# Layer 1's gate rows: bias loaded into the gates' own place, two-part rows with one-pass turns, and the eight blocks placed differently around the pooled sums

## The reference

```
def modulation(cond, w_mod, b_mod):
    m = jax.nn.silu(cond) @ w_mod + b_mod
    return jnp.split(m[..., None, :], N_MOD, axis=-1)
...
ml = modulation(c, p["w_mod"], p["b_mod"])
hl = modulate(xl, ml[0], ml[1])
dl = pool_mixer(hl, p)
xl = layer_norm(ALPHA * xl + ml[2] * dl, p["ln1_g"], p["ln1_b"])
fl = sq_relu_mlp(modulate(xl, ml[3], ml[4]), p["w_up"], p["w_down"])
xl = layer_norm(ALPHA * xl + ml[5] * fl, p["ln2_g"], p["ln2_b"])
...
def pool_mixer(h, p):
    u = h @ p["w_in"]
    pooled = multiscale_pool(u).reshape(nb, L, N_POOL_GROUPS, POOL_GROUP_DIM)
    mixed = jnp.einsum('blgc,gce->blge', pooled, p["pool_w"].astype(jnp.float32))
    mixed = mixed.reshape(nb, L, D_MODEL).astype(h.dtype) * p["pool_scale"]
    return mixed @ p["w_out"]
```

## Time and profile before

| | us |
|---|---|
| median of 3 runs | 1493.04 (1492.63 to 1494.13) |
| the profiled execution | 1491.82 |
| its span | 1489.9 |
| PE busy | 1424.0 (96%) |
| PE weight load busy | 1263.0 (85%) |
| DVE busy | 1049.6 (70%) |
| ACT busy | 550.3 (37%) |
| POOL busy | 82.7 (6%) |

### The profile page before, as it was taken

The page is one execution under the profiler, slowest core; times in us unless marked ns, Lnnn a source line. Parts: engine busy times, 40 slices in busy tenths (PEclk is TensorE's granted clock), DMA queues, the critical chain, the costliest instruction groups (busy, mean ns, idle before and its releaser), DMA issues.

```text
span 1489.9 us, 23009 instructions
## 1 busy us (share of the span) xinstructions
PE 1424.0 (96%) x8916; PEld 1263.0 (85%) x8916; DVE 1049.6 (70%) x1686; ACT 550.3 (37%) x993; POOL 82.7 (6%) x145
## 2 busy tenths in 40 slices
PE   4999999899899999999999989989999999999996
PEld 3899998666688988998999879868899899889985
DVE  3694566677667976776776795756797677677678
ACT  3333352266436422332332244443643233223322
POOL 1300000010101000000000010001100000000001
PEclk8999999999999999999999999999999999999998
DMA  9701233586722412312221522561242232223141
GB/s 314 221 29 58 85 120 122 168 273 205 268 85 68 145 57 85 114 60 83 84 85 57 211 75 67 175 202 57 71 142 59 83 114 69 74 84 94 63 167 71
DMA packets 130940, 173.80 MB, mean 117 GB/s; under 512 B 3666, under 2 KB 103370, under 8 KB 130850
## 3 DMA queue, kind: packets, MB, share of 16 engines
q1 hardware_dynamic: 123106, 146.57, 30.6%
q0 software_dynamic: 6928, 23.34, 4.8%
q10 hardware_dynamic: 816, 2.65, 0.5%
HBM read 163.63 MB, written 8.91 MB: 116 GB/s over the span
## 4 chain that ended last, share of the span: by engine, by line
PE 81%; DVE 10%; ACT 3%; issue 3%; DMA 2%; POOL 0%; SPq 0%; ACTq 0%; DVEq 0%
PE ps L721 37%; PE ps L1224 20%; PE ps L703 7%; PE ps L712 6%; PE ps L756 3%; DVE convT L1883 2%; DVE wlo L1797 2%; PE ps L1065 1%; PE ps L1088 1%; DVE acc L2244 1%; PE ps L1076 1%; DMA vec_rows<-in_b_mod_l 1%; DMA raw<-in_w_mod_l 1%; DVE gated L2255 1%; DMA raw_pool<-in_w_out_l 1%
## 5 line engine op out<-in xcount | busy, mean ns | idle before, releaser
L1336 ACT ACTIVATE whi<-raw 128x512 fp32r<-128x512 f32 (+2 forms) x186 | 175.4, 953 | 369.0 <-PE ps L721 307.0
L721 PE MATMUL ps<-whi,hid_hi 128*128 128x512 f32 x640 | 249.6, 390 | 0.0
L721 PE MATMUL ps<-wlo,hid_hi 128*128 128x512 f32 x640 | 249.2, 389 | 0.0
L721 PE MATMUL ps<-whi,hid_lo 128*128 128x512 f32 x640 | 249.0, 389 | 0.0
L1797 DVE TENSOR_TENSOR wlo<-raw,whi 128x512 fp32r<-128x512 f32 (+2 forms) x186 | 201.8, 1094 | 25.2 <-ACT whi L1336 21.6
L2237 DVE TENSOR_TENSOR acc<-acc,ps 128x512 f32<-128x512 f32 x120 | 80.3, 684 | 121.8 <-PE ps L721 121.8
L721 PE MATMUL ps<-whi,h_hi 128*128 128x256 f32 (+1 forms) x480 | 156.8, 327 | 4.6 <-DVE h_lo L2572 2.6
L721 PE MATMUL ps<-whi,h_lo 128*128 128x256 f32 (+1 forms) x480 | 152.9, 318 | 0.0
L721 PE MATMUL ps<-wlo,h_hi 128*128 128x256 f32 (+1 forms) x480 | 152.8, 318 | 0.0
L721 PEld LDWEIGHTS ps<-whi,hid_hi 128*128 128x128 f32 x640 | 120.1, 188 | 25.2 <-DVE wlo L1797 0.8
L721 PEld LDWEIGHTS ps<-whi,hid_lo 128*128 128x128 f32 x640 | 120.2, 188 | 25.0
(11 more groups left out here) (335 smaller groups left out, 2753.2 us busy)
## 6 DMA issues: line engine op xcount, KB each, us to landing
raw<-in_w_mod_l SPq DMA_DIRECT2D x39, 1024.0 KB, 5.3
raw<-in_w_up_l SPq DMA_DIRECT2D x32, 1024.0 KB, 5.6
raw<-in_w_down_l SPq DMA_DIRECT2D x32, 1024.0 KB, 5.0
raw<-in_w_in_l SPq DMA_DIRECT2D x12, 1024.0 KB, 5.3
raw_att<-in_w_mod_l SPq DMA_DIRECT2D x5, 1024.0 KB, 7.5
raw<-in_w_out_l SPq DMA_DIRECT2D x5, 1024.0 KB, 5.0
x_spill<-x_tok POOLq DMA_DIRECT2D x10, 512.0 KB, 3.0
x_tok<-x_spill POOLq DMA_DIRECT2D x10, 512.0 KB, 6.0
```

The lines of the kernel that those rows point to most:

```text
L721: mm = pe.matmul(out, a_of(still, k), w_of(part, k), start=(first and k == 0 and part == 0 and still == 0), stop=(last and k == nk - 1 and ...
L1336: act.activation(ring_piece(whi, w, g), piece(w, g), ACT.Copy).then_inc(hi_done, 1)
```

## The change

- POOL no longer clears and loads `bmod`. Instead it loads the bias of each half of layer 1's gates, broadcast to all partitions, straight into `gate`: two loads of 512 KB behind the token rows' fetch in layer 0's MLP, two behind the norms ahead of layer 1.
- The bias matmul goes. Rows of layer 1's gates are split in two as layer 0's are, with a low half `rowlo[1]` of their own, and turned by four one-pass matmuls. DVE adds the turned row to the bias in `gate`, in place; ACT's copies go.
- A table sets the places: block 40's product at n = 6, turn 40 and product 41 at n = 7, nothing at n = 8 and 9, then one turn and one product each from n = 10 to 15. Turn 47 follows the first token tile of the output projection, and the third tile waits for it.
- DVE has places too: the row difference of block 40 ahead of the last pooled sum, the addition of 40 and the difference of 41 behind it and behind the low part of the sixth sum, and the others behind each low part of the pooled projection.

```
+        TAIL = {6: (None, 40), 7: (40, 41), 10: (41, 42), 11: (42, 43), 12: (43, 44), 13: (44, 45), 14: (45, 46), 15: (46, 47)}
...
+            def preset_gate(half):
+
+                for c in range(2):
+                    pool.dma_start(gate[:, 1 - half, c, :],
+                                   A["b_mod_l1"][(2 + 3 * half) * D:(3 + 3 * half) * D].partition_broadcast(P)).then_inc(ld_gb, 16)
...
                 fetch_x_again(layer)
+                if layer == 0:
+                    preset_gate(0)
...
             norm_share(1)
+            pool.wait_ge(acc_ok[0], 80)
+            preset_gate(1)
...
-                gates = m in gate_blocks and layer == 1
-                if gates:
-                    pe.matmul(ps[0:32, b * 512:b * 512 + BW],
-                              ident[:, 24 * layer + blk:24 * layer + blk + 1].to_broadcast([P, 32]), bmod[:],
-                              start=True, stop=False)
...
-                if m in first_gates:
-                    pe.wait_ge(row_lo, m - first_gates[0] + 1)
+                if m in gate_blocks:
+                    pe.wait_ge(row_lo, m - G0 + 1)
                     pe.wait_ge(mod_out, m)
                     for c in range(2):
-                        for part, rows in enumerate((modrow_r[:, m % 2, :], rowlo[:])):
+                        for part, rows in enumerate((modrow_r[:, m % 2, :], rowlo[m // M_TAIL][:])):
...
-                if m in gate_blocks:
-                    for c in range(2):
-                        mm = pe.matmul(bank(b, c * BW, (c + 1) * BW), selr[:, c, :].bitcast(F32),
-                                       modrow[:, m % 2, :], start=True, stop=True)
...
-                pe.wait_ge(mod_out, M_TAIL if layer == 0 else 48)
+                pe.wait_ge(mod_out, M_TAIL if layer == 0 else 47)
...
                             pe.wait_ge(px_lo, KT)
+                            if t == 1:
+                                mod_turn(47)
+                            if t == 2:
+                                pe.wait_ge(mod_out, 48)
...
             def tail_mods(n):
-                m = M_TAIL + n - 6
-                if M_TAIL < m <= 48:
-                    mod_turn(m - 1)
-                if M_TAIL <= m <= 47:
+                turned, m = TAIL.get(n, (None, None))
+                if turned is not None:
+                    mod_turn(turned)
+                if m is not None:
                     mod_product(m)
...
+            def tail_rows(n):
+                if n in TAIL:
+                    mod_rows(TAIL[n][1])
...
+                    dst = gate[:, 1 - j // 3, :, q * BW:(q + 1) * BW]
+                    bias = gbias[:, j // 3, q * BW:(q + 1) * BW].unsqueeze(1).to_broadcast([P, 2, BW])
+                    dve.tensor_tensor(dst, bank(bk).rearrange("p (c n) -> p c n", c=2), (bias, dst)[layer], ALU.add) \
                         .then_inc(mod_out, 1)
...
                 split_lo(W_OUT[layer] + 1)
                 if layer == 1:
+                    mod_finish(47)
...
+            def tail_gates(n):
+                turned, m = TAIL.get(n, (None, None))
+                if turned is not None:
+                    mod_finish(turned)
+                if m is not None:
+                    row_low(m)
...
             for f in range(KT):
+                if f == 7:
+                    tail_gates(6)
                 pooled(f)
...
+            tail_gates(7)
             pooled_low(KT - 1)
             for f in range(KT):
...
                     .then_inc(px_lo, 1)
+                tail_gates(KT + f)
```

More of the change, by code:

```diff
@@ L133, in build @@
     gate_blocks = [m for m, k in enumerate(mod_k) if (S[k][2] // 4) % 3 == 2]
-    first_gates = [m for m in gate_blocks if S[mod_k[m]][1] == 0]
+    G0 = gate_blocks[0]
     ctx = ExitStack()
@@ L175, in build @@
         modrow = at("modrow", 203.6875, [P, 2, BW])
-        bmod = at("bmod_rows", 205.6875, [P, BW])
         modrow_r = at("modrow_r", 203.6875, [P, 2, BW], F32R)
-        rowlo = at("mod_row_lo", 147, [P, BW], F32R)
+        rowlo = [at(f"mod_row_lo{n}", kb, [P, BW], F32R) for n, kb in enumerate((147, 194.5))]
         selr = at("sel_r", 200.5, [P, 2, P], F32R)
@@ L551, in _ @@
         def _(pool):
-            pool.memset(bmod[:], 0.0).then_inc(zeros, 1)
             pool.memset(cpad[:], 0.0).then_inc(zeros, 1)
             pool.memset(halfp, -0.5).then_inc(zeros, 1)
-            pool.wait_ge(zeros, 1)
-            for l in range(2):
-                pool.dma_start(bmod[24 * l:24 * l + 24, :], A[f"b_mod_l{l}"].rearrange("(b n) -> b n", n=BW)) \
-                    .then_inc(ld_bm, 16)
             for n, name in enumerate(("lam_q1_l0", "lam_k1_l0", "lam_q2_l0", "lam_k2_l0")):
@@ L561, in _ @@
             steps = [0]
-            pool.wait_ge(zeros, 3)
+            pool.wait_ge(zeros, 2)
             def rsqrt(dst, src, n, scale, done):
@@ L738, in mod_product @@
                 b = 6 if m < M_MIX else 7
-                _, layer, blk = S[mod_k[m]]
                 raw_ready(pe, mod_k[m])
@@ L756, in mod_product @@
                     mm = pe.matmul(ps[32 * g:32 * g + 32, b * 512:b * 512 + BW], cpad[:, k, :],
-                                   raw_block(mod_k[m])[:, k * BW:(k + 1) * BW], start=(k < 4 and (k > 0 or not gates)), stop=(k >= 4))
+                                   raw_block(mod_k[m])[:, k * BW:(k + 1) * BW], start=(k < 4), stop=(k >= 4))
                 mm.then_inc(mod_main, 1)
@@ L773, in mod_turn @@
                     pe.wait_ge(mod_out, m)
-                if m >= M_TAIL:
-                    pe.wait_ge(mod_out, m)
-                if m in gate_blocks:
-                    for c in range(2):
-                        mm = pe.matmul(bank(b, c * BW, (c + 1) * BW), selr[:, c, :].bitcast(F32),
-                                       modrow[:, m % 2, :], start=True, stop=True)
-                else:
-                    for n in range(2):
-                        mm = pe.transpose(bank(b, n * P, (n + 1) * P), modrow[:, m % 2, n * P:(n + 1) * P], ident)
+                for n in range(2):
+                    mm = pe.transpose(bank(b, n * P, (n + 1) * P), modrow[:, m % 2, n * P:(n + 1) * P], ident)
                 mm.then_inc(mod_tr, 1)
@@ L1342, in mod_rows @@
                     act.wait_ge(mod_tr, m - 1)
-                act.activation((modrow_r if m in first_gates else modrow)[:, m % 2, :], bank(b, 0, BW), ACT.Copy) \
+                act.activation((modrow_r if m in gate_blocks else modrow)[:, m % 2, :], bank(b, 0, BW), ACT.Copy) \
                     .then_inc(mod_row, 1)
@@ L1702, in _ @@
             last_norms(1, W_IN1)
-            def gate_rows(m):
-                _, layer, blk = S[mod_k[m]]
-                j, q = blk // 4, blk % 4
-                act.wait_ge(mod_tr, m + 1)
-                act.activation(gate[:, 1 - j // 3, :, q * BW:(q + 1) * BW], bank(6).rearrange("p (c n) -> p c n", c=2),
-                               ACT.Copy).then_inc(mod_out, 1)
-            def tail_gates(n):
-                m = M_TAIL + n - 6
-                if M_TAIL <= m <= 47:
-                    mod_rows(m)
-                if M_TAIL < m <= 48:
-                    gate_rows(m - 1)
+            def tail_rows(n):
+                if n in TAIL:
+                    mod_rows(TAIL[n][1])
             def evac_u(f, hf):
@@ L1745, in _ @@
                     split_hi(W_IN1 + (f + 3) // 2)
-                tail_gates(f)
+                tail_rows(f)
             pool_high(KT - 1)
@@ L1806, in mod_finish @@
                 if m in gate_blocks:
-                    if m == first_gates[0]:
-                        dve.wait_ge(ld_gb, 16 * 2)
-                    dve.tensor_tensor(gate[:, 1 - j // 3, :, q * BW:(q + 1) * BW],
-                                      bank(bk).rearrange("p (c n) -> p c n", c=2),
-                                      gbias[:, j // 3, q * BW:(q + 1) * BW].unsqueeze(1).to_broadcast([P, 2, BW]), ALU.add) \
+                    if q == 0:
+                        dve.wait_ge(ld_gb, (32, 64 + 32 * (j // 3))[layer])
+                    dst = gate[:, 1 - j // 3, :, q * BW:(q + 1) * BW]
+                    bias = gbias[:, j // 3, q * BW:(q + 1) * BW].unsqueeze(1).to_broadcast([P, 2, BW])
+                    dve.tensor_tensor(dst, bank(bk).rearrange("p (c n) -> p c n", c=2), (bias, dst)[layer], ALU.add) \
                         .then_inc(mod_out, 1)
@@ L2188, in _ @@
                     evac_z(8 * NT - 2 + a)
-                if a != SKIP:
-                    row_low()
+                if a != SKIP and todo[0] < M_TAIL:
+                    row_low(todo[0])
                 if a < NT:
```

26 lines of the change are left out of this document (11 added, 15 removed).

## The result

Over 20 runs of each, the kernel before took 1492.51 us (median) and the changed one 1494.36 us. The ratio is **1.0019**, with a 95% interval of 1.0011 to 1.0026: 2.8 us slower, between 1.6 and 3.9 (the two medians are 1.85 us apart). That is just inside the 0.2% that I had called no difference, and outside zero. The profiled execution of the changed kernel has a span of 1492.7 us, that of before 1489.9.

A forecast was written before the change was run, and what follows sets the result against it. PE was taken as the bound, except where ACT waits for the first output block's load. Less PE work (-6.9) against longer idle and a clock fall gave 3.0, plus 0.55 for turn 47: +3.5 us, 1496.5, range 1493.0 to 1499.8.

The forecast's parts named there:

- A load issued before 970 us: Sign against the forecast: the first output block's 1 MB load, expected to go out at 971.0, leaving before 970 us.
- Parts 1 to 4: Layer 1's gate blocks: 6.9 us less PE work, 0.25 us waiting for DVE, 1.9 us more idle before pool step 2.
- Part 5: Ahead of turn 44: ACT waits for the first output block's load, issued later and taking 7.3 us; 7.1 us more PE idle.
- Part 6: Behind the 8.8 us stop: PE's clock falls to half, costing 2.3 us, 0.5 of it covered; nothing behind the 2.3 us idle.
- Part 7: End of the stretch: wait ahead of the output projection 1.0 us shorter; turn 47 costs 0.55 us inside the projection.
- what was costed at nothing: Four 512 KB bias broadcasts on POOL's queue, the dropped memset and small loads, and ACT's lost copies: no time either way.
- A: Rival, no measurable difference: clock loss covered by existing waits, load landing a little sooner; 1493.8 to 1494.8 us, chance 30%.
- B: Rival, faster: load landed by 970.6, when ACT's row copy of block 44 is due; gain 7.6 us, 1485.4, chance 10%.
- C: Rival, slower still: both idle times drop the clock and the load takes 8.8 us; 6.8 us slower, 1499.8, chance 10%.

The follow-up runs named there:

- e6: The kernel before with only the changed kernel's new places for the gate work, old bias matmul, fp32 turns and gate copies kept; ratio to before 1.0046.
- e1: The changed kernel with the first output block's load moved from behind modulation block 46 to ahead of block 44; 1484.11 us, ratio to before 0.9950.
- e9: The changed kernel with the first output block's load one place earlier only, ahead of modulation block 46; ratio to before 0.9995.
- e7: The changed kernel with the load ahead of block 44 and ACT emptying pool step 0's bank before the last pooled sum's high part; ratio to before 0.9941.
- e5: The kernel before with the first output block's load moved ahead of modulation block 45; ratio to before 0.9993.
- e10: The changed kernel with each pair of 512 KB bias loads issued twice, eight broadcasts instead of four; ratio to before 1.0018.
- e4: The changed kernel with 60 further matmuls, results unused, keeping PE busy ahead of turn 44; ratio to before 1.0014.
- e2: The changed kernel with gate work at the old places, behind pool steps 0 to 5, turn 47 staying in the projection; 1493.19 us, ratio to before 1.0012.
- e3: The changed kernel with ACT copying block 44's row ahead of the output block's high part instead of behind it; ratio to before 1.0014.

## Why the prediction was right, and where it was off

The forecast was +3.5 us, the runs say +2.8 (1.6 to 3.9), and the mechanism is the one forecast. The sum itself has a flaw: its terms give 3.65 us, 4.2 with turn 47, while the times of the steps give 2.9 and 3.5. The prediction called this rounding, which it is not, and went by the steps; the trace has the +4.2 of the terms. Step by step, with the prediction's times on the scale of the kernel before: the last block of `u` starts at 945.80 there and at 944.03 in the changed kernel, which the prediction had 0.41 us sooner, so 1.36 is added to the changed kernel's times.

| step | predicted | measured |
|---|---|---|
| start of pool step 2, idle ahead of it | 960.05, 2.3 | 959.98, 2.09 |
| end of step 5, where PE stops | 972.3 | 972.56 |
| load issued | 971.0 | 971.13 |
| load's duration | 7.3 | 8.12 |
| turn 44, idle ahead of it | 981.1, 8.8 | 982.01, 9.45 |
| projection starts, idle ahead of it | 993.5, 1.6 | 994.20, 1.33 |
| turn 47 in the projection | 0.55 | 0.48 |

"A load issued before 970 us" was to be a sign of a wrong prediction. In the changed kernel's own time it was issued at 969.77, on the scale on which the prediction reckoned at 971.13.

**Parts 1 to 4** held: eight products and turns lighter by 0.41 us each, rounds of 3.4 to 3.7 us that now and then wait for DVE, 2.1 us ahead of step 2. Taking the changed idle times (+1.67, +7.69 and -1.27 us), the half clock (+2.0) and the longer projection (+0.55) out of the trace's +4.20 leaves -6.4 us for the lighter work, where 6.65 was counted (6.9 - 0.25). Between e6 and the changed kernel it is 5.5 us; 0.7 of the difference is the idle time ahead of step 2, 1.37 us in e6 and 2.09 in the changed kernel.

**Part 5** is the term that was mis-sized. The load was the cause, as e1 and e9 show, but I took the duration from the pair with nothing behind it, 7.3, where this load took 8.12. Over all kernels here it took 5.1 and 5.4 us where no other load had been issued in the 6 us ahead of it (e1, e7), and 6.9 to 9.3 where a block's load was issued up to 0.9 us ahead: 6.9 in e5, 7.44 in e10, 7.45 in e9, 8.12 in the changed kernel, 8.21 in e4, 8.49 in e2, 8.64 in e6, 8.80 before and 9.29 in e3. What stands behind it, by which I chose 7.3 over 8.8, does not sort them: without a load behind it that falls in its time it took 7.44 to 8.64 (e10, changed, e4, e6), with one 6.9 to 9.29 (e5, e9, e2, before, e3). My range of 5.2 to 8.8 was right for the changed kernel; a single value to a tenth was more than the rows gave. The Trainium skill's DMA: Bandwidth & Descriptors (Anatomy of one DMA) would make it 4.4 us as an estimate, for GpSimd's transfers. The trace of e1, 5.1 us alone, is the nearest to it, and a load with another just ahead of it took 1.8 to 4.2 us more than that.

**Part 6**: the clock fell behind the long stop and not behind the 2.09 us, both as taken. Its cost of 2.3 us with 0.5 covered, 1.8 net, measured 1.56 in e4: 2.0 us, with 0.4 covered. The Trainium skill's advice in TensorE: Matmul & The Clock Gate (Why this matters for your kernels), to avoid idle gaps between bursts, holds here in the sense that the gap cost this on top of its own length; e4 bought it back with unused work; e1 removed the gap itself, which is worth 10.2 us with the clock in it.

**Part 7 and what was costed at nothing** held within 0.3 us; the projection takes 60.59 us to the restart in the MLP, against 60.04 before, so no wait was added at its third tile. e10 is the test of the bias loads.

**The rivals.** The time alone would speak for A. Its range of 1493.8 to 1494.8 contains the median, 1494.36; my own figure of 1496.5 lies 2.1 above it, and the median is under the forecast's own range too, 1495.0 to 1498.0. Part of the gap is the base: the median of before over 20 runs is 0.5 us under that of the three I had. As differences from the base the forecast's range is +2.0 to +5.0 and A's +0.8 to +1.7; the ratio's 2.8 is in the first, the 1.85 between the medians is in neither. What decides is the trace, which contradicts A's mechanism twice: the load landed later than forecast and not sooner, and the fall was not covered. B's point, the load landed ahead of ACT's need, is what e1 builds, and it gained 7.5 us by the ratio where B said 7.6. C did not occur.

**What stays open.** The trace says +4.2 us, the runs +2.8. For every kernel of the table the runs put the difference to before 0.7 to 2.8 us below the distances, so the profiled execution of before seems a short one in this stretch. A possible reason is in e5: behind the 2.60 us ahead of the projection the clock can fall, at 1.6 us, and in the profiled execution of before it did not. That other executions of before lose it there was not shown; each kernel has one trace. That executions of one kernel differ by the clock can be seen in the runs: of the changed kernel's 20, the 7 with a mean granted clock of 0.987 average 1493.1 us and the 13 with 0.983 to 0.985, the profiled one (0.984) among them, 1495.6.

## What to carry to other kernels

When work is moved past a fixed point of another engine's queue, look up which transfer that point waits for and what issues it: here the blocks were moved two steps later, the load's issue went with them, and ACT's place for it did not. Follow each edit through every in-order queue that the released instruction depends on, DVE's as well as ACT's; e3 lost its whole gain to the one that was left out. With the lighter gate work at its new places, the cheap remedy is one block moved in the stream, and the table of buffers with it: e1 is 0.5% faster than before and 0.7% faster than the change without it. With the old work at the old places the same remedy brought nothing clear (e5). Whether it would do as much with the new content at the old places was not tried.

Two edits that meet in one chain of waits have no separate prices: the new places cost 9.7 us by the trace with the old gate work and 0.25 with the new. Build all four corners before saying what each half is worth.

## What the runs showed that was not expected

The length of an idle time alone did not tell whether the clock falls. In the stretch it fell behind 2.68 us (e2, ahead of 981.96) and behind 2.60 us (e5), and stayed at 1.00 behind 2.60 us in the kernel before, behind 2.60 us in e2 (ahead of 992.76) and behind 2.09 us in the changed kernel. Ahead of the restart in the MLP all kernels idle for 2.64 to 2.66 us, and the clock fell behind it in ten of the eleven traces; in e1 it stayed up:

```profile
1046.00:1050.00 4.00, 3.52 (x26) 3.25 (x26) 3.86 (x8) 1.24 (x1) 2.08 (x3) 1.00 0.00 1
```

In layer 0 all kernels idle for 2.28 or 2.29 us near 373 us, and the clock fell behind it in eight traces and stayed at 1.00 in e4, e5 and e10. A window of the changed kernel, and one of e4:

```profile
373.00:377.00 4.00, 4.00 (x32) 3.42 (x27) 2.63 (x11) 1.69 (x8) 0.00 (x0) 0.64 1.09 366
```

```profile
374.00:378.00 4.00, 4.00 (x49) 2.94 (x49) 3.35 (x13) 2.27 (x8) 0.00 (x0) 1.00 1.08 366
```

From there to a restart near 455 us the eight take 82.2 to 82.4 us and the three 80.8, and the three have the earliest landmarks of all. So the cost of one fall could be isolated three times, and it was about 1.6 us each time: behind the long stop (1.56, e4 against the changed kernel), behind 2.60 us (1.59, e5 against before) and here (1.4 to 1.7).

The same 1 MB load took between 5.1 and 9.3 us, a spread as large as everything else that this change moved.
